# Token-major products of 512 weight columns written as two of 256 into the halves of one bank, with the high and low parts of the moving operand at one address modulo 512

## The reference

```python
h = rmsnorm(x, pre_norm_g[l])
(u, v, z_a, c_q, c_kv, k_rope, z_b, x_c, z_c, g_a, g_b, g_c) = jnp.split(h @ w_in[l], cuts, axis=-1)
y_a = gmlp_spatial(u, v, ...) * silu(z_a)
y_b = mla_attention(c_q, c_kv, k_rope, ...) * silu(z_b)
y_c = rg_lru(x_c, ...) * silu(z_c)
merged = (sigmoid(g_a) * (y_a @ w_proj_a[l]) + sigmoid(g_b) * (y_b @ w_proj_b[l])
          + sigmoid(g_c) * (y_c @ w_proj_c[l]))
x = x + rmsnorm(merged @ w_out[l], post_norm_g[l])
```

```python
x = x + (silu(g) * a) @ ffn_down[i]                 # a, g: halves of conv(rmsnorm(x) @ ffn_up[i])
x = x + sigmoid(rmsnorm_2(x, norm_ple[i]) @ ple_gate[i]) * (p[i] @ ple_proj[i])
```

## The kernel before, in words

| operand | before |
|---|---|
| h_hi, h_lo | 224, 224 |
| c, h2, ya, yb, yc, y2, p, high and low | 480, 480 |
| w_hi, buffers 0 to 5, slots of 512 columns | 224 352 352 480 480 96 |
| w_lo, the same | 96 224 224 352 352 480 |
| w_hi, slots of (8, 256) and of the queries | 288 288 416 416 32 32 |
| w_lo, the same | 160 160 288 288 416 416 |

## Time and profile before

### The profile page before, as it was taken

How to read it: one execution, slowest core, us unless ns; L and a number is a source line. 1 busy time by engine, 2 the same in 40 slices (tenths; PEclk the granted TensorE clock), 3 DMA queues, 4 the chain that set the end, 5 groups by cost and what they waited for, 6 DMA issues and landing times.

```text
span 1452.0 us, 23083 instructions
## 1 busy us (share of the span) xinstructions
PE 1421.6 (98%) x9283; PEld 1282.3 (88%) x9283; DVE 1050.5 (72%) x1601; ACT 867.3 (60%) x1522; POOL 91.5 (6%) x154
## 2 busy tenths in 40 slices
PE   8999999999999999999999999999999999999997
PEld 8999999787789999998878799988899888999886
DVE  7747679986676466799866788874776745888746
ACT  7574766564464747665644666654775544766545
POOL 9100000007000100000000000000000000000000
PEclk9999999999999999999999999999999989999999
DMA  8743576566556435765565457755535003666553
GB/s 255 195 117 117 157 209 202 174 189 196 189 158 176 118 118 153 219 196 175 190 230 181 130 177 217 220 187 179 163 104 160 30 1 120 201 197 193 183 180 116
DMA packets 189851, 242.29 MB, mean 167 GB/s; under 512 B 19343, under 2 KB 134211, under 8 KB 189745
## 3 DMA queue, kind: packets, MB, share of 16 engines
q1 hardware_dynamic: 183232, 228.66, 51.8%
q0 software_dynamic: 6416, 12.13, 2.9%
q10 hardware_dynamic: 96, 0.03, 0.0%
HBM read 238.42 MB, written 1.05 MB: 165 GB/s over the span
## 4 chain that ended last, share of the span: by engine, by line
PE 88%; ACT 5%; DVE 4%; DMA 2%; issue 1%; DVEq 0%; SPq 0%
PE bank L635 26%; PE bank L638 25%; PE bank L639 25%; PE bank L1242 2%; PE bank L856 1%; PE bank L855 1%; ACT w_hi L1347 1%; ACT T L1857 1%; DVE w_lo L1916 1%; DMA raw<-in_w_in 1%; PE bank L1199 1%; PE bank L1156 1%; PE bank L1228 1%; ACT S L1552 1%; PE bank L760 1%
## 5 line engine op out<-in xcount | busy, mean ns | idle before, releaser
L1916 DVE TENSOR_TENSOR w_lo<-raw,w_hi 128x1024 fp32r<-128x1024 f32 (+2 forms) x452 | 518.5, 1170 | 226.2 <-ACT w_hi L1347 223.1
L1347 ACT CAST w_hi<-raw 128x1024 fp32r<-128x1024 f32 (+2 forms) x452 | 449.3, 1009 | 269.1 <-DMA raw<-in_w_in 116.4
L635 PE MATMUL bank<-h_hi,w_hi 128*128 128x256 f32 (+1 forms) x1640 | 455.8, 278 | 6.6 <-DVE h_lo L1952 4.2
L638 PE MATMUL bank<-h_lo,w_hi 128*128 128x256 f32 (+1 forms) x1640 | 453.6, 277 | 0.0
L639 PE MATMUL bank<-h_hi,w_lo 128*128 128x256 f32 (+1 forms) x1640 | 453.2, 276 | 0.0
L635 PEld LDWEIGHTS bank<-h_hi,w_hi 128*128 128x128 f32 (+1 forms) x1640 | 306.4, 187 | 9.8 <-issue 7.9
L638 PEld LDWEIGHTS bank<-h_lo,w_hi 128*128 128x128 f32 (+1 forms) x1640 | 306.5, 187 | 0.1
L639 PEld LDWEIGHTS bank<-h_hi,w_lo 128*128 128x128 f32 (+1 forms) x1640 | 306.4, 187 | 0.0
L635 PE MATMUL bank<-w_hi,h_hi 128*128 128x512 f32 (+1 forms) x464 | 178.7, 385 | 1.9 <-issue 1.0
L638 PE MATMUL bank<-w_lo,h_hi 128*128 128x512 f32 (+1 forms) x464 | 176.6, 381 | 0.0
L639 PE MATMUL bank<-w_hi,h_lo 128*128 128x512 f32 (+1 forms) x464 | 176.6, 381 | 0.0
(11 more groups left out here) (368 smaller groups left out, 2126.3 us busy)
## 6 DMA issues: line engine op xcount, KB each, us to landing
raw<-in_w_in SPq DMA_DIRECT2D x160, 512.0 KB, 3.9
raw<-in_ffn_up SPq DMA_DIRECT2D x88, 512.0 KB, 4.4
raw<-in_ffn_down SPq DMA_DIRECT2D x40, 512.0 KB, 4.5
raw<-in_w_proj_a SPq DMA_DIRECT2D x16, 512.0 KB, 3.5
raw<-in_w_proj_b SPq DMA_DIRECT2D x16, 512.0 KB, 3.6
raw<-in_w_proj_c SPq DMA_DIRECT2D x16, 512.0 KB, 3.7
raw<-in_w_out SPq DMA_DIRECT2D x16, 512.0 KB, 3.6
raw<-in_ple_gate SPq DMA_DIRECT2D x16, 512.0 KB, 4.7
```

Of the source, the lines that this page charges most:

```text
L635: first = pe.matmul(out_, lh, rh, start=start, stop=False)
L638: pe.matmul(out_, lh, rl, start=False, stop=False)
L1347: act.copy(weights(w_hi, slot, b, size), weights(raw, slot, b, size)).then_inc(sems["hi_done"], 1)
L1916: dve.tensor_tensor(weights(w_lo, slot, b, size), weights(raw, slot, b, size), weights(w_hi, slot, b, size).bitcast(F32), ALU.subtract).th ...
```

## The change

A helper `wide_three(bank, n, ...)` runs over n in steps of 256 columns and calls `three` for each step, the first into columns 0 to 255 of the bank and the second into 256 to 511. The `start` flag and `w_begun` go with the first step, `stop` with the last. It takes the place of `three` in `tokens`, `tokens_in_turn`, `ple_product`, `gate_by_token` and `project2`. `keys_values` keeps its wide products.

The buffers are laid anew. w_hi uses `place(slot)` in every buffer and w_lo `SHIFT - place(slot)`, so that with the new base addresses both parts of a wide slot have one remainder. h_hi and h_lo stand in rooms that are 16 elements longer than they, so that each can be used at two places: `h` as before, and `s` (s_hi, s_lo) moved by 64 bytes. s is used for the products of w_out, of ple_gate and of the second attention's output, and ScalarE and VectorE write it in these places. The spaces between other tiles change so that ya, yb, yc, y2 and p get new remainders:

| operand | after, modulo 512 |
|---|---|
| h_hi, h_lo | 352, 352 |
| s_hi, s_lo | 416, 288 |
| ya, yb, y2: high, low | 288, 160 |
| yc: high, low | 160, 32 |
| p: high, low | 32, 416 |
| c, h2, high and low | 96, 96 |
| w_hi and w_lo, buffers 0 to 5, slots of 512 columns, both | 352 480 96 224 352 480 |
| w_hi, slots of (8, 256) and of the queries | 416 32 160 288 416 32 |
| w_lo, the same | 288 416 32 160 288 416 |

To find the room, the mask `causal1` is kept at half its size and `rec` is dropped: the recurrence works in place in I, with one more wait on VectorE's own semaphore `dve_step`.

```diff
-            first = place(slot) if b % 2 == 0 else SHIFT - place(slot)
+            first = place(slot) if t is w_hi else SHIFT - place(slot)
...
+            def wide_three(bank, n, lh, ll, rh, rl, start, stop, begins=False):
+
+                for c0 in range(0, n, TOK):
+                    cols = slice(c0, c0 + TOK)
+                    mm = three(ps[bank][:, cols], lh, ll, rh[:, cols], rl[:, cols], start and c0 == 0, stop and c0 == n - TOK, begins and c0 == 0)
+                return mm
...
-                            mm = three(ps[banks[t]][:, 0:n], hi, lo, weights(w_hi, slot, b)[:, cols], weights(w_lo, slot, b)[:, cols],
+                            mm = wide_three(banks[t], n, hi, lo, weights(w_hi, slot, b)[:, cols], weights(w_lo, slot, b)[:, cols],
...
-        h_hi = sb("h_hi", [P, KT, TOK], F32R)
-        h_lo = sb("h_lo", [P, KT, TOK], F32R)
+        h_hi, s_hi, h_lo, s_lo = h_view(0, 0), h_view(0, SHIFT), h_view(1, SHIFT), h_view(1, 0)
...
-                tokens_in_turn([(0, 0), (1, 4)], 0, h)
+                tokens_in_turn([(0, 0), (1, 4)], 0, s)
...
-                dve.tensor_tensor(xc[:, t, :], xc[:, t, :], I[:, t, :], ALU.mult)
-                ins_ = dve.tensor_scalar(rec[:, :, :], R[:, t, :], 1.0, None, ALU.add)
+                dve.tensor_tensor(xc[:, t, :], xc[:, t, :], I[:, t, :], ALU.mult)\
+                    .then_inc(sems["dve_step"], w.given("dve_step"))
+                dve.wait_ge(sems["dve_step"], w.value("dve_step"))
+                ins_ = dve.tensor_scalar(I[:, t, :], R[:, t, :], 1.0, None, ALU.add)
```

More of the change, by code:

```diff
@@ L261, in kb, with steps @@
             return (None, [P, 256 * n], F32)
+        def steps(n):
+            return (None, [P, SHIFT * n], F32)
         cst = sb("cst", [P, NCONST])
@@ L724, in tokens_in_turn @@
                                 cols = slice((k - ka) * n, (k - ka + 1) * n)
-                                mm = three(ps[bank][:, 0:n], hi, lo, weights(w_hi, slot, b)[:, cols], weights(w_lo, slot, b)[:, cols],
+                                mm = wide_three(bank, n, hi, lo, weights(w_hi, slot, b)[:, cols], weights(w_lo, slot, b)[:, cols],
                                            k0 + k == 0, (j, k) == (parts[-1][0], k_tiles - 1),
@@ L810, in keys_values @@
                     mm.then_inc(sems[f"full{bank}"], 1)
-            h = (h_hi, h_lo)
+            h, s = (h_hi, h_lo), (s_hi, s_lo)
             TWO = [plain(0), plain(P)]
@@ L1008, in ple_product @@
                         cols = slice(n * 512, (n + 1) * 512)
-                        mm = three(ps[bank][:, :], hi, lo, weights(w_hi, w.n["S"], bs_[k])[:, cols], weights(w_lo, w.n["S"], bs_[k])[:, cols],
+                        mm = wide_three(bank, 512, hi, lo, weights(w_hi, w.n["S"], bs_[k])[:, cols], weights(w_lo, w.n["S"], bs_[k])[:, cols],
                                    k == 0, k == 1, u == 3)
@@ L1079, in piece @@
                         tok, cols = slice(t * P, (t + 1) * P), slice((k - ka) * 512, (k - ka + 1) * 512)
-                        three(ps[banks[t]][:, :], h_hi[:, k, tok], h_lo[:, k, tok], weights(w_hi, slot, b)[:, cols],
+                        wide_three(banks[t], 512, s_hi[:, k, tok], s_lo[:, k, tok], weights(w_hi, slot, b)[:, cols],
                               weights(w_lo, slot, b)[:, cols], k == 0, False, k == ka and (half == 0) == (t == 0))
@@ L1271, in project2 @@
                             cols = slice(n * 512, (n + 1) * 512)
-                            mm = three(ps[bank][:, :], h_hi[:, k, t * P:(t + 1) * P], h_lo[:, k, t * P:(t + 1) * P],
+                            mm = wide_three(bank, 512, s_hi[:, k, t * P:(t + 1) * P], s_lo[:, k, t * P:(t + 1) * P],
                                        weights(w_hi, slot, b)[:, cols], weights(w_lo, slot, b)[:, cols], k == 0, k == KT - 1, begins)
@@ L1426, in split_token @@
                     at = (k // 2) * P
-                    act.activation(h_hi[:, k, t * P:(t + 1) * P], ps[b][:, at:at + P], ACT.Identity, scale=gain(k))\
+                    act.activation(s_hi[:, k, t * P:(t + 1) * P], ps[b][:, at:at + P], ACT.Identity, scale=gain(k))\
                         .then_inc(sems["ht_hi"], w.given("ht_hi"))
@@ L1966, in low_token @@
                     dve.wait_ge(sems["ht_hi"], w.taken("ht_hi"))
-                    dve.scalar_tensor_tensor(h_lo[:, k, tok], ps[b][:, at:at + P], gain(k), h_hi[:, k, tok].bitcast(F32),
+                    dve.scalar_tensor_tensor(s_lo[:, k, tok], ps[b][:, at:at + P], gain(k), s_hi[:, k, tok].bitcast(F32),
                                              ALU.mult, ALU.subtract).then_inc(sems["ht_ready"], w.given("ht_ready"))
@@ L2333, in low_merged @@
                         dve.wait_ge(sems["m_hi_done"], w.taken("m_hi_done"))
-                        dve.tensor_tensor(h_lo[:, k:k + 2, :].rearrange("p a n -> p (a n)"), ps[b][:, :],
-                                          h_hi[:, k:k + 2, :].rearrange("p a n -> p (a n)").bitcast(F32), ALU.subtract)\
+                        dve.tensor_tensor(s_lo[:, k:k + 2, :].rearrange("p a n -> p (a n)"), ps[b][:, :],
+                                          s_hi[:, k:k + 2, :].rearrange("p a n -> p (a n)").bitcast(F32), ALU.subtract)\
                             .then_inc(free[b], 1)
@@ L2725, in low_o @@
                 dve.wait_ge(sems["o_hi_done"], w.taken("o_hi_done"))
-                dve.tensor_tensor(flat(h_lo[:, 2 * g:2 * g + 2, :]), ps[b][:, :],
-                                  flat(h_hi[:, 2 * g:2 * g + 2, :]).bitcast(F32), ALU.subtract)\
+                dve.tensor_tensor(flat(s_lo[:, 2 * g:2 * g + 2, :]), ps[b][:, :],
+                                  flat(s_hi[:, 2 * g:2 * g + 2, :]).bitcast(F32), ALU.subtract)\
                     .then_inc(free[b], 1)
```

65 lines of the change are left out of this document (35 added, 30 removed).

## The result

The changed kernel takes 1459.89 us (median of 18 runs, 1452.47 to 1465.53), the kernel before in the same sessions 1449.47 us (median of 18). The forecast was a gain of 2.1 us; it came out as a loss of some 9. The profiled execution took 1461.46 us, its span is 1459.7 us against 1452.0.

What follows compares the result with a forecast made beforehand. TensorE was taken as the bound, time being number of products times the distance between their starts. Terms -7.6 + 5.4 + 0.1 gave -2.1 us, so 1452.3 us, with a range of 1443 to 1462.

Steps and rivals of the forecast that it cites:

- What bounds the kernel: Whole kernel: TensorE busy 98% of the 1452.0 us span, so time is number of products times distance between starts.
- Term (1): 560 wide triples with ya, yb, yc, y2, p or s stationary: cut pair 226.6 ns against 231.1, -7.6 us.
- forecast A: Wide products: addresses decide the spacing and plain-h products are slow; own range 1447 to 1461 us, chance 0.47.
- Term (2): 256 triples with plain h stationary: cut pair 238.0 ns against 231.0, as in keys and values, +5.4 us.
- rival B: Plain-h products are fast as well, since only aligned moving parts count: 1443.5 us, chance 0.25.
- Term (3): Wide stages: 2448 more weight loads, covered by the product in flight, priced at 0.
- Term (4): Recurrence with one tile fewer: L2036 waits for the product reading I, some 0.12 us later, +0.1 us.
- Rival C: Halves of wide products: a toll of 6.6 ns per instruction, 118.9 ns each, +16.2 us, 1471; chance 0.15.
- Rival D: Wide streams: a column costs 0.45 ns however cut, 115.5 ns for 256 columns, 1454.5 us; chance 0.13.

Runs made afterwards that it cites:

- the kernel in which nothing moves: Changed kernel with the stream of 512-column slots at one address modulo 256 in all buffers, y, s, p cut, plain h uncut: 1444.57 us, ratio 0.9932 against before.

## Why the prediction was wrong, point by point

**What bounds the kernel: right.** TensorE is at 98% in both, and distance times number explains most of the difference. By the triples the sum of the change is: y and p, 400 x (2 x 348.5 - 692.8) = +1.7 us; s, 160 x (2 x 349.1 - 692.9) = +0.8; plain h +5.8; the narrow products of h, 1568 x (340.3 - 341.3) = -1.6; the recurrence +0.1. Together +6.8 us, where the spans differ by 7.7 and 0.6% is 8.7.

**Term (1) is the step that failed.** It gave the pair 226.6 ns, -7.6 us, since FFN up stands at the same relation. The relation had been read modulo 128, and modulo 256 it is two relations. FFN up has both of them and holds 340 in both, so its row could not warn; its stream stands still, and that was not seen as a condition. With a stream that moves, the half of the pieces at (192, 64) takes 356 ns: (341.5 + 356) / 2 = 349 per half, 232.5 ns per pair and +2.5 us. The warning stood in the earlier trace rows, and the text named it ("narrow products at times run for some microseconds at another spacing"), but used its stretch's mean, 115.7, as a bound. The term came out at 116.3, beyond even that bound. So the time of 1459.9 us lies in forecast A's own range, at the end that term (1) reaches at its worst bound: the danger was named, and what was wrong is that it was taken for an exception. The right question to the earlier trace rows would have been what put the products into that spacing, and whether the change does that at each piece.

**Term (2), +5.4 us: right**, +5.8 measured. The keys row was the right neighbour: aligned parts at distance 0 give 119 to 120 ns. That both stationary parts lie at the stream's address does not help at 256 columns (360 ns a triple), so rival B is out; at 512 columns this place is the best one seen (680).

**Term (3), 0: right.** In FFN down of the kernel in which nothing moves, loads are busy 40.00 of 40.00 us, and products still follow each other at 113.1 ns.

**Term (4), +0.1 us: right.** VectorE of the kernel after, to be held against the earlier trace rows:

```profile
205.34 0.42 DVE L2051 TENSOR_TENSOR xc<-xc,I 128x256 f32<-128x256 f32 x1
205.79 0.29 DVE L2054 TENSOR_SCALAR I<-R 128x256 f32<-128x256 f32 x1
206.12 1.75 DVE L2058 RECIPROCAL I<-I 128x256 f32<-128x256 f32 x1
```

The second instruction starts 0.45 us behind the first, where it was 0.34.

**Not in the sum:** the narrow products of h gained 1.6 us. In the kernel before 106 of their triples at (192, 64) stood in the slow spacing, in the kernel after none, with the same relations; at which stalls the slow spacing sets in has changed. **Rival C** would have given 118.9 in all halves and 1471. As a toll it is refuted: 356 products of half the width fit where 178 fit. **Rival D**, that a column costs the same however it is cut, is right in the best places and wrong as a forecast, because the cut moves the best place.

The Trainium skill's rule ("TensorE: Matmul & The Clock Gate", section "Back-to-back issue gap"), by which the prediction had estimated 1460.5 us, came within a microsecond of the result, but not by its reason: cut and uncut in their best places are 226.2 and 226.9 ns for 512 columns by the counts (226.7 for both by the triples), where a fixed 2.5 ns for each product would make the cut dearer by 2.5. The Trainium skill says in the same section that its formula is for an isolated product, and gives about 131 ns for 512 columns in a stream of loads and products; no row here comes near this.

What stays open is what the addresses collide in. That 340 and 680 ns are steady at several places and 353/360 is a second steady state at one would fit two periodic accesses that fall into step or out of it, but this is a guess and no run tests it. Nor was it tried by itself whether a stream that moves by 64, and not by 128, disturbs. It happens twice in the kernel with plain h's weights moved by 64 (at 312.62 and 715.95 us, into yb at (192, 64)), and there the triples are 354 or 355, 351, 341 and then 340.

## What to carry over

Read a spacing from a neighbour only if everything about the neighbour is the same, also what does not change from one piece to the next: the good row had a stream that stood still. When the same code shows two spacings in one trace, find out what switches them before the change is priced; a few microseconds of it can be the steady state of the kernel after. And part a change that does two things: here the cut was worth nothing and the placement some 10 us, 0.7%, and the kernel in which the stream has the same place modulo 256 in every buffer, with nothing cut at all, beats both kernels (1444.87 us, 0.9931).

## What the runs showed of the chip

- With fp32r operands in three products of one step, 512 columns take between 226.7 and 233 ns and 256 columns between 113.3 and 121 ns on the mean, by the addresses of the operands and by whether the stream's address moves, at a granted clock of 1.00 (2.4 GHz).
- The best place of those tried depends on the width: 512 columns want both stationary parts at the stream's address modulo 256 (680 ns; 695.5 where they are 64 and 192 past it), 256 columns want them there where 512 don't (340; 360 at the stream's address).
- TensorE has a memory in this: at (192, 64) one move of the stream by 128, or some stalls, leave it 4 to 5% slower (118.6 against 113.5 ns) for as long as nothing changes, 44 us and 20 pieces at the longest that was seen.
